# One channel group's taps straight after its gating: a depthwise convolution shared by TensorE and VectorE in a two-layer streaming encoder

## The reference

```python
def conv_glu(h, w_pw1, b_pw1):
    a, g = jnp.split(jnp.einsum('btd,dc->btc', h, w_pw1) + b_pw1, 2, axis=-1)
    return a * jax.nn.sigmoid(g)

def conv_rest(u_ext, w_dw, b_dw, ln_g, ln_b, w_pw2):
    y = lax.conv_general_dilated(u_ext, w_dw[:, None, :], ..., feature_group_count=CONV_CH) + b_dw
    y = jax.nn.silu(layer_norm(y, ln_g, ln_b))
    return jnp.einsum('btc,cd->btd', y, w_pw2)
```

## Time and profile before

| | us |
|---|---|
| median of 3 runs | 1005.0 |
| lowest and highest of them | 1003.52, 1007.41 |
| the profiled execution, its own time | 1006.78 |
| the profiled execution, span of the trace | 1005.0 |
| mean granted TensorE clock, share of full speed | 0.952 |
| TensorE matmul busy | 878.0 (87%) |
| VectorE busy | 326.9 (33%) |
| ScalarE busy | 209.3 (21%) |

### The profile page before, as it was taken

How to read it: one execution, slowest core, us unless ns; L and a number is a source line. 1 busy time by engine, 2 the same in 40 slices (tenths; PEclk the granted TensorE clock), 3 DMA queues, 4 the chain that set the end, 5 groups by cost and what they waited for, 6 DMA issues and landing times.

```text
span 1005.0 us, 14051 instructions
## 1 busy us (share of the span) xinstructions
PE 878.0 (87%) x5438; PEld 515.3 (51%) x5438; DVE 326.9 (33%) x794; ACT 209.3 (21%) x448; POOL 81.7 (8%) x93
## 2 busy tenths in 40 slices
PE   6999999999899878788859999759999978878783
PEld 5888888788533323232345555338863333323222
DVE  1514453424411101010142888861351111101013
ACT  3413244223111011010131223341111101010110
POOL 1100000000011111111000000000001101111100
PEclk9999999999899999999968999879989999999997
DMA  9713611329969999999975122304357999999955
GB/s 348 313 45 131 169 53 45 153 80 412 414 261 417 420 419 420 419 420 414 382 305 214 77 85 85 111 1 188 144 191 283 418 419 420 419 418 419 419 239 202
DMA packets 47714, 271.12 MB, mean 270 GB/s; under 512 B 10693, under 2 KB 10845, under 8 KB 18904
## 3 DMA queue, kind: packets, MB, share of 16 engines
q1 hardware_dynamic: 34416, 239.66, 58.9%
q0 software_dynamic: 11600, 24.27, 7.0%
q10 hardware_dynamic: 1632, 6.29, 1.7%
HBM read 266.54 MB, written 25.37 MB: 290 GB/s over the span
## 4 chain that ended last, share of the span: by engine, by line
PE 60%; DMA 29%; DVE 6%; SPq 2%; issue 2%; ACT 1%; ACTq 0%; POOLq 0%; DVEq 0%
DMA slot<-in_experts 24%; PE PS L577 12%; PE PS L993 10%; PE PS L1084 9%; PE PS L1016 7%; PE PS L830 6%; PE PS L807 2%; PE PS L974 2%; PE PS L1101 2%; DMA outs<-Y,IDX 2%; DMA XGT<-rows,IDX 2%; DMA slot<-outs 1%; SPq L379 1%; PE PS L935 1%; PE PS L887 1%
## 5 line engine op out<-in xcount | busy, mean ns | idle before, releaser
L993 PE MATMUL PS<-slot,XG 128*64 128x512 f32 x1024 | 247.0, 629 | 67.0 <-DMA slot<-in_experts 65.0
L993 PEld LDWEIGHTS PS<-slot,XG 128*64 128x64 f32 x1024 | 80.1, 143 | 210.2 <-issue 194.0
L1749 DVE SCALAR_TENSOR_TENSOR hid_by_token<-PS,SC,SG 128x256 f32<-128x256 f32 x32 | 15.5, 484 | 397.1 <-ACT SG L1325 397.1
L577 PE MATMUL PS<-slot,HT 128*128 128x256 f32 x576 | 132.6, 386 | 7.7 <-ACT HT L1165 7.7
L577 PEld LDWEIGHTS PS<-slot,HT 128*128 128x128 f32 x576 | 108.1, 192 | 25.1 <-ACT HT L1165 9.1
L1016 PE MATMUL PS<-slot,HID 128*64 128x512 f32 x512 | 116.3, 596 | 0.9 <-ACT HID L1330 0.9
L1084 PE MATMUL PS<-HC,slot 128*128 128x384 f32 x256 | 89.1, 505 | 1.6 <-DVE HC L1825 1.6
L1325 ACT ACTIVATE SG<-PS,SC 128x256 f32<-128x256 f32 x32 | 15.2, 475 | 269.3 <-PE PS L993 269.3
L1084 PEld LDWEIGHTS PS<-HC,slot 128*128 128x128 f32 x256 | 49.1, 196 | 41.7 <-issue 11.8
L1339 ACT ACTIVATE Y<-PS,SC 128x1024 f32<-128x1024 f32 x32 | 35.7, 1114 | 153.6 <-PE PS L1016 153.6
L1016 PEld LDWEIGHTS PS<-slot,HID 128*64 128x64 f32 x512 | 34.6, 137 | 57.3 <-issue 55.9
(11 more groups left out here) (291 smaller groups left out, 806.5 us busy)
## 6 DMA issues: line engine op xcount, KB each, us to landing
slot<-in_experts SPq DMA_DIRECT2D x192, 1024.0 KB, 22.2
slot<-in_w_pw SPq DMA_DIRECT2D x12, 1024.0 KB, 8.2
slot<-in_w_in SPq DMA_DIRECT2D x11, 1024.0 KB, 10.9
slot<-outs ACTq DMA_DIRECT2D x6, 1024.0 KB, 7.2
slot<-in_w_out SPq DMA_DIRECT2D x4, 1024.0 KB, 7.7
rows<-X POOLq DMA_DIRECT2D x6, 512.0 KB, 8.7
KTC<-in_k_past POOLq DMA_DIRECT2D x1, 2048.0 KB, 13.7
slot<-in_v_past SPq DMA_DIRECT2D x2, 1024.0 KB, 8.4
```

What stands on the lines that cost most here:

```text
L577: last = mm(PS[:, in_bank(n), 0:UCOL], HT[:, k, P * t:P * (t + 1)], w[:, k, :], start=k == 0, stop=k == KD - 1)
L993: last = mm(PS[CAP * e:CAP * (e + 1), 2 + p % 2, :], XG[:, p % 2, k, CAP * e:CAP * (e + 1)], w[:, 2 * FE * (k % 4):2 * FE * (k % 4 + 1)], ...
```

## The change

Five things are edited.

1. **VectorE's order.** `gated(c)` now stands directly ahead of group c's own taps, and the next group's `diagonals` between the two. The addition of TensorE's part is a function of its own, `folded(c)`, and comes one group later.
2. **The split of taps.** `ROUNDS` becomes a table, 3, 3, 2, 3, 2, 3, 3, 4: VectorE takes 19, 19, 23, 19, 23, 19, 19, 15 taps.
3. **TensorE's end.** `taps(6)` moves ahead of `glu_half(7, 1)`; the sums for the mean are written in three places, three of them before `taps(7)` and four behind it. ScalarE no longer copies the fold of groups 6 and 7: VectorE adds them from the bank.
4. **The sigmoid's table** is loaded by a small extra instruction before the first sigmoid.
5. **The norm's last steps** go by token tiles: root in two pieces (tokens 0 to 127, 128 to 383), reciprocal and product tile by tile (the first tile's product in two halves), silu in 24 pieces of 128 by 128 instead of 8 of 128 by 384. `z_ready` counts to 24, and SyncE's wait for it with it.

Some pairs of semaphores that count the same kind of event are also merged into one each (`qt_act` and `kt_act`, `gl_exp` and `d_exp`, `mean_done` and `var_done` among them); outside the convolution that moves no instruction.

```diff
@@ -50,8 +50,8 @@
 PBLK = SEQ // LS
 STRIP = 32
 NSTRIP = P // STRIP
-ROUNDS = 3
-PE_TAPS = ROUNDS * NSTRIP
+ROUNDS = (3, 3, 2, 3, 2, 3, 3, 4)
+PE_TAPS = [r * NSTRIP for r in ROUNDS]
 UNIT = 2048
 LO, HI, SLOTS = 6, 12, 16
 RINGS = ((12, 13, 14, 15, 0, 1, 6, 7, 8, 9, 10, 11, 2, 3, 4, 5), (6, 7, 8, 9, 10, 11, 0, 1, 12, 13, 14, 15, 2, 3, 4, 5))
@@ -438,7 +438,7 @@
             sp.wait_ge(S("glu_done"), KD)
             for q in range(6, 8):
                 expert_load(1, q)
-            sp.wait_ge(S("z_ready"), KD)
+            sp.wait_ge(S("z_ready"), KD * NT)
             sp.wait_ge(S("stored"), 16 * (STATE_STORES + CONV_STORES))
             for q in range(8, 12):
                 expert_load(1, q)
@@ -825,8 +825,8 @@
                         full(seg, first + u)
                     w = dense(first + u)
                     for k in range(ks):
-                        if parts and u == t == 0:
-                            pe.wait_ge(S(parts), k + 1)
+                        if parts and u == 0 and (t == 0 or k == 0):
+                            pe.wait_ge(S(parts), KD * (t + 1) if t else k + 1)
                         last = mm(PS[:, RING[i % 4], UCOL * (u % 2):UCOL * (u % 2) + UCOL], lhs[:, k, P * t:P * (t + 1)],
                                   w[:, k, :], start=k == 0, stop=k == ks - 1)
                 last.then_inc(S("out_done"), 1)
@@ -1091,15 +1091,17 @@
 
                 pe.wait_ge(S("uhist_ready"), c + 1)
                 pe.wait_ge(S("diag_ready"), c + 1)
-                if c:
+                if c == KD - 1:
+                    pe.wait_ge(S("y_conv"), c)
+                elif c:
                     pe.wait_ge(S("fold_out"), c)
-                for m in range(ROUNDS):
+                for m in range(ROUNDS[c]):
                     for i in range(NSTRIP):
                         rows = slice(STRIP * i, STRIP * (i + 1))
                         for j in range(NSTRIP):
                             w = NSTRIP * m + j
                             last = mm(PS[STRIP * j:STRIP * (j + 1), 4 + i, 0:TOK], DG[rows, c % 2, w, :],
-                                      U[rows, c, :, w:w + LS], start=m == 0, stop=m == ROUNDS - 1,
+                                      U[rows, c, :, w:w + LS], start=m == 0, stop=m == ROUNDS[c] - 1,
                                       skip_group_check=True, tile_position=(STRIP * i, STRIP * j))
                 last.then_inc(S("taps_done"), 1)
 
@@ -1116,22 +1118,34 @@
             glu_half(0, 1)
             glu_half(1, 0)
             glu_half(1, 1)
-            for c in range(KD):
+            for c in range(KD - 2):
                 taps(c)
-                if c + 2 < KD:
-                    glu_half(c + 2, 0)
+                glu_half(c + 2, 0)
                 fold(c)
-                if c + 2 < KD:
-                    glu_half(c + 2, 1)
-
-            for c in range(KD):
+                if c == KD - 3:
+                    taps(c + 1)
+                glu_half(c + 2, 1)
+            fold(KD - 2)
+
+            def mean(c):
+
                 pe.wait_ge(S("y_conv"), c + 1)
                 last = mm(PS[:, 0, 0:TOK], C["onesd"], YC[:, c, :], start=c == 0, stop=c == KD - 1)
-            last.then_inc(S("mean_done"), 1)
+                if c == KD - 1:
+                    last.then_inc(S("mean_done"), 1)
+
+            pe.wait_ge(S("u_ready"), KD - 1)
+            for c in range(3):
+                mean(c)
+            taps(KD - 1)
+            for c in range(3, KD - 1):
+                mean(c)
+            fold(KD - 1)
+            mean(KD - 1)
             for c in range(KD):
                 pe.wait_ge(S("ysq_ready"), c + 1)
                 last = mm(PS[:, 1, 0:TOK], C["onesd"], YS[:, c, :], start=c == 0, stop=c == KD - 1)
-            last.then_inc(S("var_done"), 1)
+            last.then_inc(S("mean_done"), 1)
             def conv_projected(t, h):
                 out_half("c", 8, YC, 1, t, h, "z_ready")
 
@@ -1377,6 +1391,7 @@
                 q.do(A(SGC[:, c % 2, :], PS[:, 2 * (c % 2) + 1, 0:TOK], ACT.Sigmoid, bias=SMT[:, 8 + c:9 + c]),
                      S("sig_ready"))
 
+            preload(ACT.Sigmoid)
             sigmoids(0)
             for c in range(KD):
 
@@ -1387,7 +1402,7 @@
                 q.link(A(stat[:, 12:13], C["eps"], ACT.Copy), S("uhist_ready"))
                 q.do(A(UN[:, c, :].rearrange("p (b l) -> p b l", b=NS), U[:, c, PBLK:, HIST:], ACT.Copy),
                      S("unew_ready"))
-                if c + 1 < KD:
+                if c + 2 < KD:
                     sigmoids(c + 1)
                 act.wait_ge(S("taps_done"), c + 1)
                 if c >= 2:
@@ -1396,21 +1411,28 @@
                     q.do(A(RS[:, c % 2, 2 * half:2 * half + 2, :], PS[:, 4 + 2 * half:6 + 2 * half, 0:TOK], ACT.Copy))
                 q.settle()
                 q.link(A(stat[:, 12:13], C["eps"], ACT.Copy), S("strips_out"))
-                act.wait_ge(S("fold_done"), c + 1)
-                if c >= 2:
-                    act.wait_ge(S("y_conv"), c - 1)
-                q.do(A(FO[:, c % 2, :], PS[:, 4, 0:TOK], ACT.Copy), S("fold_out"))
+                if c + 2 == KD:
+                    sigmoids(c + 1)
+                elif c + 2 < KD:
+                    act.wait_ge(S("fold_done"), c + 1)
+                    if c >= 2:
+                        act.wait_ge(S("y_conv"), c - 1)
+                    q.do(A(FO[:, c % 2, :], PS[:, 4, 0:TOK], ACT.Copy), S("fold_out"))
             preload(ACT.Sqrt)
             for c in range(KD):
                 act.wait_ge(S("yc_centred"), c + 1)
                 q.do(A(YS[:, c, :], YC[:, c, :], ACT.Square), S("ysq_ready"))
-            act.wait_ge(S("var_done"), 1)
-            q.link(A(VR[:, :], PS[:, 1, 0:TOK], ACT.Sqrt, bias=C["eps"]), S("cstd_ready"))
+            act.wait_ge(S("mean_done"), 2)
+            for cols in (slice(0, P), slice(P, TOK)):
+                q.do(A(VR[:, cols], PS[:, 1, cols], ACT.Sqrt, bias=C["eps"]), S("cstd_ready"))
             preload(ACT.Silu)
-            for c in range(KD):
-                act.wait_ge(S("yc_normed"), c + 1)
-                q.do(A(YC[:, c, :], YC[:, c, :], ACT.Silu, scale=SMT[:, 24 + c:25 + c], bias=SMT[:, 32 + c:33 + c]),
-                     S("z_ready"))
+            for t in range(NT):
+                cols = slice(P * t, P * (t + 1))
+                for c in range(KD):
+                    if c == 0 or t == 0 and c == 4:
+                        act.wait_ge(S("yc_normed"), t + 2 if t else 1 + c // 4)
+                    q.do(A(YC[:, c, cols], YC[:, c, cols], ACT.Silu, scale=SMT[:, 24 + c:25 + c],
+                           bias=SMT[:, 32 + c:33 + c]), S("z_ready"))
             moe(1, extra0)
 
 
@@ -1837,20 +1859,31 @@
 
                 if c >= 2:
                     dve.wait_ge(S("taps_done"), c - 1)
-                q.do(V.tensor_tensor(DG[:, c % 2, :, :], bc(C["strip"], 1, PE_TAPS),
-                                     bc(WDT[:, c, 0:PE_TAPS], 2, STRIP), ALU.mult), S("diag_ready"))
+                q.do(V.tensor_tensor(DG[:, c % 2, 0:PE_TAPS[c], :], bc(C["strip"], 1, PE_TAPS[c]),
+                                     bc(WDT[:, c, 0:PE_TAPS[c]], 2, STRIP), ALU.mult), S("diag_ready"))
+
+            def folded(c):
+
+                if c + 2 < KD:
+                    dve.wait_ge(S("fold_out"), c + 1)
+                    part = FO[:, c % 2, :]
+                else:
+                    dve.wait_ge(S("fold_done"), c + 1)
+                    part = PS[:, 4, 0:TOK]
+                q.do(V.tensor_tensor(YC[:, c, :], YC[:, c, :], part, ALU.add), S("y_conv"))
 
             diagonals(0)
-            gated(0)
             for c in range(KD):
+                gated(c)
                 if c + 1 < KD:
                     diagonals(c + 1)
-                    gated(c + 1)
+                else:
+                    folded(c - 1)
                 dve.wait_ge(S("uhist_ready"), c + 1)
 
                 accs, sides = (blocks(YC[:, c, :]), blocks(YD[:, :])), (S("conv_a"), S("conv_b"))
-                for w in range(PE_TAPS, CONV_W):
-                    n = w - PE_TAPS
+                for w in range(PE_TAPS[c], CONV_W):
+                    n = w - PE_TAPS[c]
                     acc, side = accs[n % 2], sides[n % 2]
                     if side is sides[1] and n < 2 and c:
                         dve.wait_ge(S("conv_sum"), c)
@@ -1866,18 +1899,22 @@
                     q.do(ins, side)
                 q.settle()
                 q.link(V.tensor_tensor(YC[:, c, :], YC[:, c, :], YD[:, :], ALU.add), S("conv_sum"))
-                dve.wait_ge(S("fold_out"), c + 1)
-                q.do(V.tensor_tensor(YC[:, c, :], YC[:, c, :], FO[:, c % 2, :], ALU.add), S("y_conv"))
+                if 1 <= c < KD - 1:
+                    folded(c - 1)
+            folded(KD - 1)
             q.settle()
             dve.wait_ge(S("mean_done"), 1)
             for c in range(KD):
```

(11 more changed lines are left out.)

32 lines of the change are left out of this document (16 added, 16 removed).

## The result

The change runs in 993.35 us, median of 4 runs (989.29 to 995.74), against 1004.26 for the kernel before beside it (1000.26 to 1007.41, 4 runs). The ratio is 0.9900 with a 95% interval of 0.9876 to 0.9923: 10.9 us faster. Run again later, it came to 993.5 against 1002.5, ratio 0.9923 (0.9896 to 0.9950). 10.1 was forecast. In that later set one run of this kernel (1265.9 us) and one of the kernel without the early table load (1267.9 us) fell into a slow state with a granted clock of 0.65; the medians given here leave both out.

What follows compares the result with a forecast made beforehand. It took VectorE's late convolution taps, then the norm's one-link chain, as the bound; 7.3 (VectorE's order) + 0.9 (mean) + 1.9 (root to projection) = 10.1 us, from 1005.0 to 994.9, rounded 995; range 990.5 to 999.

Steps and rivals of the forecast that it cites:

- VectorE's chain sets the end, and the order costs it one group: End of the convolution: VectorE's taps run one group late because the next gating stands ahead of them; reordering gains 7.3 us.
- The recorded walk: Sum of taps and waits along VectorE's stream to its last addition: 660.4 in the old order, 653.1 in the new.
- The head start is mostly spent: VectorE in the convolution: waiting for group 1's history idles it 6.8 us, most of the head start.
- TensorE is ready in time: End of the convolution: TensorE waits 1.5 and 1.8 us ahead of groups 6 and 7; last fold 1.2 ahead of VectorE's last tap.
- Mean: Norm, last sum of the mean on TensorE: at full clock 0.8 us instead of 1.66, 0.9 gained.
- Variance: Norm, variance entries: 6.86 us before, possibly 5.4 or 10.2 by the clock; no change taken.
- the clock helps: Rival, chance 0.18: variance and projection at full clock gain 1.5 + 2.6 us more, 990.8.
- Root to projection: Norm's last steps, root's start to projection's start: 2.85 us instead of 4.77 by token tiles, 1.9 gained.
- eight pieces of at most 0.31: ScalarE's silu pieces behind the projection's start: each at most 0.31 us against eight matmuls at 0.43, so TensorE isn't starved.
- Projection's clock: Projection's first 96 entries: 2.6 us lost to the low clock before; might be saved, or 2.5 more lost; no change taken.
- Carried to the end one to one: Behind the projection: the rest follows rigidly, so a gain at the projection's start reaches the end in full.
- a sign of being wrong if the expert stage's length changed by more than 1: Expert stage, paced by its loads: a length changed by more than 1 us would show the forecast wrong.

Runs made afterwards that it cites:

- two rounds: The change with two rounds for every group, so VectorE takes 23 taps everywhere and TensorE 8: 1002.35 us, ratio 1.0009 to the kernel before.
- history first: The change with each group's history copied on ScalarE ahead of the wait for the previous group's fold: 987.99 us, ratio 0.9860 to the kernel before.
- unfilled gaps: Kernels without extra matmuls in TensorE's three idle gaps of the norm; the change itself is one, at 993.35 us.
- gaps were filled: The change with matmuls that change no value added in TensorE's three norm gaps: 992.63 us with 4, 3 and 8, 990.6 us with 2, 1 and 4.
- with three: The change with three rounds for every group, twelve taps on TensorE everywhere: 996.75 us, ratio 0.9944 to the kernel before.
- second trace: The change itself, unaltered, run and profiled again: 993.5 us, ratio 0.9923 to the kernel before; its variance took 8.28 us against 7.16 in the first.

## Why the prediction was right, point by point

- **VectorE's chain sets the end, and the order costs it one group.** Right. 7.2 measured for 7.3 forecast; the waits 6.87, 2.19 and then under 0.8 stand where they were put. The recorded walk gave the differences of all five orders and splits that were run within 0.35, also with two rounds, where the gain turns around. The chain behind one of them was wrong all the same: with history first the total came out (2.9 for 3.1), while neither wait was as expected.
- **The head start is mostly spent.** Right, and shown by two runs: 1.28 more of it is worth nothing, and moving the history ahead of ScalarE's wait is worth 2.9.
- **TensorE is ready in time.** Right: 1.50 and 1.54 of idling ahead of the taps of groups 6 and 7 (forecast 1.5 and 1.8), last fold 1.1 ahead of the last addition. The clock didn't fall in that wait.
- **Mean.** 0.7 for 0.9: the last sum took 0.93, not 0.77.
- **Variance.** 0 forecast, 0.3 lost in the first trace, 1.4 in the second. I took no change since the gap directly ahead is the same 1.3. In seven executions of kernels with the change's order at the end and unfilled gaps the variance took 5.5 to 8.5, six of them at 6.95 or more, so a small loss was the likelier guess, and the prediction had no means to tell. The range held it. Of "the clock helps", both halves came true only where the gaps were filled.
- **Root to projection.** 1.8 for 1.9, 2.98 for 2.85 in length. The path was the forecast one, over ScalarE: two root pieces, the table load of 1.28 and its first use, with silu beginning at 2.34 for 2.4 (the prediction's own terms add up to 2.24). The rest of the miss is the silu piece, 0.50 on the chain for 0.31, since its price came from a plain copy. The reciprocal took 0.95, as taken. The term "eight pieces of at most 0.31" failed; the pieces come each 0.39, and were still hidden.
- **Projection's clock.** 0 forecast, 0.7 gained here and 2.4 in the traces with three and with two rounds. The guess was as open as the variance's.
- **Carried to the end one to one.** Not contradicted: from the first taps to the routing's end the difference is 10.2. But the prediction called it a sign of being wrong if the expert stage's length changed by more than 1, and it changed by 3.1. That bound was too tight: in executions of kernels that share this stage the stretch took 264.8 to 268.4, so one pair of traces can neither show nor exclude a difference of 1 there.
- **The sum.** 10.1 forecast and 10.2 measured to the gathering is closer than the method allows. The terms missed by 0.1 to 0.7 and cancelled, and the change's second trace gives 9.1 by the same count, since its variance took longer. What the runs support is the 7.2 of the walk, which came out in every trace of this order, and 1.8 to 2.1 for the tile-wise end.
